# A PEER expert layer: one-hot rows made one expert tile earlier, and a rehearsal of TensorE moved across a stage boundary

## What is computed

```python
def peer_ffn(h, w_query, sub_keys, expert_u, expert_v):
    ...
        v1, i1 = lax.top_k(s1, PEER_TOPK)
        v2, i2 = lax.top_k(s2, PEER_TOPK)
        ...
        eidx = e1 * PEER_N_KEYS + e2
        gate = jax.nn.softmax(top, axis=-1)
        u = expert_u[eidx]
        vv = expert_v[eidx]
        act = jax.nn.gelu(jnp.einsum('td,thkd->thk', xc, u).astype(jnp.float32), approximate=False)
        wts = (gate * act).astype(xc.dtype)
        return jnp.einsum('thk,thkd->td', wts, vv)
```

## Time and profile before

| | us |
|---|---|
| runs | 3630.94, 3632.36, 3635.39 |
| median | 3632.36 |
| the profiled execution's own time | 3639.17 |
| its span, first to last instruction | 3637.1 |
| PE busy in the span | 3529.8 (97%) |
| DVE busy | 2954.1 (81%) |
| ACT busy | 1801.0 (50%) |

### The profile page before, as it was taken

The page is one execution under the profiler, slowest core; times in us unless marked ns, Lnnn a source line. Parts: engine busy times, 40 slices in busy tenths (PEclk is TensorE's granted clock), DMA queues, the critical chain, the costliest instruction groups (busy, mean ns, idle before and its releaser), DMA issues. The chain is left out here.

```text
span 3637.1 us, 54279 instructions
## 1 busy us (share of the span) xinstructions
PE 3529.8 (97%) x19394; PEld 3093.5 (85%) x19394; DVE 2954.1 (81%) x6507; ACT 1801.0 (50%) x3462; POOL 727.3 (20%) x569
## 2 busy tenths in 40 slices
PE   8979999999999999999999999999999999999999
PEld 7558788999999988888788668789999999888887
DVE  5675654998999899999676586547998998899998
ACT  5434543335888633333444564333347888433333
POOL 0130000001333344444000000000003323344442
PEclk9889999999999999999999999999999999999999
DMA  4452323556999899999322003234558999999997
GB/s 145 199 166 89 97 76 113 164 164 213 342 328 325 310 400 398 402 400 400 138 90 87 33 30 96 95 101 127 160 167 292 336 325 321 355 401 400 402 398 298
DMA packets 371755, 853.44 MB, mean 235 GB/s; under 512 B 35728, under 2 KB 184848, under 8 KB 368912
## 3 DMA queue, kind: packets, MB, share of 16 engines
q1 hardware_dynamic: 260896, 531.17, 41.7%
q0 software_dynamic: 73728, 268.47, 19.7%
q10 hardware_dynamic: 36864, 50.35, 3.8%
HBM read 753.26 MB, written 95.42 MB: 233 GB/s over the span
## 5 line engine op out<-in xcount | busy, mean ns | idle before, releaser
L1298 POOL DMA_INDIRECT p2f_row<-in_expert_u_rows,p2f_index x128 | 169.0, 1320 | 1274.2 <-issue 1004.9
L1298 POOL DMA_INDIRECT p1f_row<-in_peer_u_rows,p1f_index x128 | 173.8, 1358 | 927.0 <-issue 661.2
L1962 PE MATMUL p1v_out<-p1a_u_hi,p1v_w_hi 128*128 128x512 f32 x768 | 299.4, 390 | 0.0
L1962 PE MATMUL p2v_out<-p2a_u_hi,p2v_w_hi 128*128 128x512 f32 x768 | 299.1, 390 | 0.0
L1962 PE MATMUL p1v_out<-p1a_u_hi,p1v_w_lo 128*128 128x512 f32 x768 | 299.0, 389 | 0.0
L1962 PE MATMUL p1v_out<-p1a_u_lo,p1v_w_hi 128*128 128x512 f32 x768 | 299.0, 389 | 0.0
L1962 PE MATMUL p2v_out<-p2a_u_lo,p2v_w_hi 128*128 128x512 f32 x768 | 298.9, 389 | 0.0
L1962 PE MATMUL p2v_out<-p2a_u_hi,p2v_w_lo 128*128 128x512 f32 x768 | 298.8, 389 | 0.0
L1462 ACT CAST p1a_u_hi<-p1a_u 128x1024 fp32r<-128x1024 f32 x128 | 135.1, 1055 | 282.9 <-PE p1v_out L1962 282.9
L1462 ACT CAST p2a_u_hi<-p2a_u 128x1024 fp32r<-128x1024 f32 x128 | 135.1, 1056 | 270.0 <-PE p2v_out L1962 270.0
L1298 POOL DMA_INDIRECT p2f_row<-in_expert_v,p2f_index x128 | 171.9, 1343 | 249.0 <-DVE p2f_sum L1321 223.6
(11 more groups left out here) (761 smaller groups left out, 10610.2 us busy)
## 6 DMA issues: line engine op xcount, KB each, us to landing
p1a_u<-in_peer_u SPq DMA_DIRECT2D x128, 512.0 KB, 4.1
p1a_u<-in_peer_v SPq DMA_DIRECT2D x128, 512.0 KB, 8.3
p2a_u<-in_expert_u SPq DMA_DIRECT2D x128, 512.0 KB, 4.4
p2a_u<-in_expert_v SPq DMA_DIRECT2D x128, 512.0 KB, 9.1
gates<-p_kept SPq DMA_DIRECT2D x20, 2048.0 KB, 15.1
acts<-p1a_a ACTq DMA_DIRECT2D x128, 192.0 KB, 4.0
p1w_a<-acts SPq DMA_DIRECT2D x128, 192.0 KB, 7.1
acts<-p2a_a ACTq DMA_DIRECT2D x128, 192.0 KB, 4.0
```

Of the source, the lines that this page charges most:

```text
L1298: self.nc.gpsimd.indirect_dma_start(self.row[:, n % self.RING, :], None, self.u_rows if dot else self.v_rows, bass.IndirectOffsetOnAxis(ap ...
L1962: last = nc.tensor.matmul(out[:, o, :], lhs[:, s, t * P:(t + 1) * P], rhs[:, n % VSLABS, cols], start=(n == 0 and m == 0), stop=(n == KEYS ...
```

## The change

VectorE's loop asks for `steps_after(i + 1)`, so that it makes in its turn i the one-hot rows that TensorE uses after tile i + 1; the upper end is clipped, so that the last turn makes none. TensorE and ScalarE keep `steps_after(i)`. At the end of TensorE's part of the gates' stage stand 12 calls of the rehearsal, into the PSUM tile `tp`, and the values' stage begins with 5 in place of 10.

```diff
         def steps_after(i):
 
-            return range(ALL * max(i - 1, 0) // (TILES - 1), ALL * i // (TILES - 1))
+            return range(ALL * max(i - 1, 0) // (TILES - 1), ALL * min(i, TILES - 1) // (TILES - 1))
...
                     A.split_lo(dve, INTO + AHEAD - 1 + i)
-                for s in steps_after(i):
+                for s in steps_after(i + 1):
...
                     last.then_inc(hot_free, 1)
+            rehearse(nc, C["ident"], tp[:].rearrange("p n k -> p (n k)"), 12)
...
         def _(pe):
-            rehearse(nc, C["ident"], out[:, 0, :])
+            rehearse(nc, C["ident"], out[:, 0, :], 5)
+
```

## The result

Twelve executions of the changed kernel have a median of 3642.38 us (3634.13 to 3645.59), twelve of the kernel before, on the same chip, 3632.64 us. The ratio is 1.0022, 95% interval 1.0014 to 1.003: 9.7 us slower, against a forecast of 11.6 us faster, and outside the range of 3615 to 3627.

The account below looks back on a forecast made before the run. The prediction took TensorE's pace to bound the gates' stage, other engines mattering only where TensorE stands still. Gains of 7.2 + 4.4 = 11.6 us, taken from the median of 3632.4, gave 3620.8 us, range 3615 to 3627.

Parts of the forecast that it names:

- One-hot rows a turn earlier: Start of both layers' gates' stages: TensorE's waits at steps 0 and 1 go, gaining 7.2 us.
- the rival of the next wait: Gates' start: ScalarE's step 1 remainder rows or the low part behind come late, half of 7.2 us stays; 3624.4 us, 9%.
- What is queued behind the earlier rows: Gates' stage: VectorE waits for ring slots a turn sooner, holding a low part and a take; costed at nothing.
- Rehearsal: Boundary from gates' to values' stage, both layers: split rehearsal brings an earlier first product and a faster clock, 4.4 us.
- the rival of clock luck: Stage boundary: if the clock stayed up in earlier timed runs, nothing is gained there; gain 7.2 us, 3625.2 us, 15%.
- The rival of the slower side: Gates' tiles: ring-slot waits hold the low part and take turn after turn, VectorE becomes the bound; 3656 us, 4%.

Follow-up runs that it names:

- first_steps: The change, but one-hot rows a tile ahead only in VectorE's first five turns, none in the sixth, then as before; 8.9 us faster than the kernel before.
- rehearse_only: The change's rehearsal edits alone, with VectorE's one-hot rows as in the kernel before; 2.5 us faster than the kernel before.
- small_stores: The change with each 2 MB store of gates cut into four of 512 KB in successive turns of SP; 8.9 us faster than the kernel before.
- hot_small: The change's earlier one-hot rows with gates' stores cut into four of 512 KB, and the old rehearsal; 4.8 us faster than the kernel before.
- hot_only: The change without its rehearsal edits, so only the one-hot rows made earlier; 9.0 us slower than the kernel before.
- act_stores: The change with the 2 MB stores of gates issued on ScalarE's queue in place of SP's; 108.7 us slower than the kernel before.

## Why the prediction was wrong, step by step

- **One-hot rows a turn earlier, 7.2 us**: right in kind, somewhat large. The starts gained 7.0, but 1.0 us came back at tiles 3 to 6 with the change and 2.0 in first_steps, where the prediction expected no wait: the rival of the next wait (9%) came in small. The 7.7 us of first_steps' stages hold 2.8 us that the moved rows did not bring.
- **What is queued behind the earlier rows, at nothing**: this step failed. It priced the wait for a slot by when TensorE needs the low part, with VectorE's spare 7% as cover. The low part's first user is not TensorE but SP: the end of the low part frees the slot of the next table load. Two things shorten the lead, from 12.2 to 9.2 us: the ring, whose waits rise from 9 to about 31 us a layer, and the 2.3 us of rows made ahead, until spare time makes them good. How the 3.0 us divide between them is not shown. Behind a 2 MB store 3 us less are too few. The change's gates' stages are 751.3 us in sum, those of first_steps 730.1: the step cost 21 us in the profiled executions, and 9.7 + 8.9 = 18.6 us by the medians.
- **Rehearsal, 4.4 us**: right in kind, too large. Against the profile of before it holds: from the last gates product to the last product of the values 530.2 and 528.9 us became 527.5 in both layers. But the six kernels with the old rehearsal (12 boundaries) show 530.2 once, 528.9 six times and 527.3 five times, while all 20 with the new one show 527.5. The mean gain is 0.9 us a boundary, 1.7 in all. By the medians the new rehearsal is worth 2.5 us (rehearse_only against before), 4.1 (small_stores against hot_small) and -0.7 (the change against hot_only), each uncertain by 3 to 5 us, so they don't settle its size. The term was measured on an execution that lost the clock in both layers, and subtracted from the median of others: the rival of clock luck, given 15%, was nearer here. The rule of the Trainium skill weighed there (TensorE: Matmul & The Clock Gate, Part 1: The HAM clock gate), that the slow matmuls at a restart vary between runs and are not to be fitted, agrees with these 12 boundaries.
- **The rival of the slower side, 4%**: its mechanism was named rightly, a wait for a ring slot that holds the low part and the take behind it. Its price was not: it counted a little in every turn once VectorE's spare is used up. VectorE never became the bound; TensorE pays at the stores, and again in half clock, 8.5 us where it was 3.4 (1.7 of either at the start of the second layer's stage, not at a stall).

## What to carry to other kernels

When work is moved ahead of other work on an engine, follow what stands behind it to its first user, which can be a transfer that waits for a buffer, and compare the time that this leaves the transfer, at the place where it is shortest, with its slowest landing, not with the median and not with the engine's busy share. A large store needs as much room on its queue as the loads behind it can spare; cutting it, or moving work ahead only where a stall is seen, kept the gain here. A gain read from one execution's clock is to be counted at the mean over several places.

## What the runs showed of the hardware

- Behind a 2 MB store on a queue, the issue of a following transfer took up to 9.6 us in place of 0.33 in the change (9.4 in the kernel before), and held its engine: SP there, ScalarE in act_stores (5.5 us on average). The Trainium skill (DMA: Bandwidth & Descriptors, Issuing engines are not separate DMA queues) says that issuing from several engines only saves the sequencer's time, usually small against the transfer. Here it was not small, and the queue did matter: the slowest load went from 16.9 to 8.9 us when the stores left its queue, in a kernel that is 3% slower.
- The Trainium skill (DMA: Bandwidth & Descriptors, Rules for kernel authors) asks for 1 MiB or more in a DMA for bandwidth. Here stores of 512 KB in place of 2 MB made the kernel 18.6 us faster than the change, since their size set the latency of the loads behind.
- A stall of TensorE of about 2 us took the granted clock to 0.50, the 1.2 GHz level, for some us in one place and not in another. With the change, two windows of 2 us from 2795.6 us on hold 0.74 and 1.39 us of idle time, and the next has a clock of 0.50; two from 2891.6 on hold 0.98 and 1.12, and the clock stays at 1.00. The first is one wait of 2.13 us, the second two waits of 1.26 and 0.84 us with products between (the columns are those of the stages above):

```profile
2795.60:2797.60 2.00, 1.26 (x9) 1.11 (x8) 2.00 (x6) 2.00 (x4) 0.00 (x0) 1.00 1.03 387
2797.60:2799.60 2.00, 0.61 (x5) 0.62 (x6) 1.89 (x3) 2.00 (x7) 0.97 (x1) 0.85 0.94 367
2799.60:2801.60 2.00, 2.00 (x7) 2.00 (x8) 1.96 (x6) 2.00 (x5) 0.70 (x1) 0.50 0.89 264
...
2893.60:2895.60 2.00, 0.88 (x9) 0.75 (x10) 1.28 (x5) 2.00 (x7) 0.55 (x1) 1.00 1.03 365
```
